# Hybrid decoder trunk on one core: the attention stage put in another order on TensorE, with its buffers moved to suit

## The chip, the cores and the metric

One core of one Trainium2 chip runs the whole program. The metric is the device time of one launch in microseconds (us), the median of three runs.

## The reference

Two pre-norm layers act on x of 256 tokens by 1024 channels, all in float32. In each layer, one projection of the normed x gives low-rank latents for multi-head latent attention (MLA: 8 heads, 96 wide queries and keys, 64 wide values), q, k and v of a dilated attention (3 groups of 8 heads, 64 wide), and two gates. Then

```python
merged = (jax.nn.sigmoid(g_mla) * (o_mla @ w_br_mla[i])
          + jax.nn.sigmoid(g_dil) * (o_dil @ w_br_dil[i]))
x = x + merged @ w_out[i]
```

Here o_mla is causal softmax attention, and o_dil is softmax attention over the three groups together with a distance bias. After it come a SwiGLU (layer 0) or the top 2 of 8 SwiGLU experts (layer 1), and a gated per-layer embedding. A last norm ends the program.

## The kernel before, in words

**Units.** All weights come from one stream in DRAM in the order in which they are used. SyncE loads slabs of 1 MB into six buffers (`raw`). A slab holds two units of 128 by 1024 numbers. ScalarE rounds each unit to fp32r (`hi`, L554), and VectorE writes what is left of it (`lo`, L925), each into a ring of four. A unit is then 12 TensorE matmuls of 512 columns (L1425 to L1427: high by high, high by low, low by high, for two blocks of 128 rows and both token tiles; with one token tile in the experts, six). ScalarE may round unit u only when TensorE has used unit u - 4 (`used`). Both engines take their work in program order, so a unit to be split can stand behind attention work, and the other way round.

**Attention stage of a layer** (the functions `attn` of each engine). The projections come first: latents, v (`U_V`), the MLA up-projections, then q and k of the dilated attention as six chunks of four units (`U_Q`, `U_K`). ScalarE copies each chunk to `chunk` (L661), TensorE transposes it in rounds (L1510), and VectorE copies the round to `qT` or `kT` (L1056). After all six chunks, 22 softmax batches follow: 6 of MLA (`NB_M`), 16 of the dilated attention. The latter come in pairs: token tile 0 with 128 keys per group, tile 1 with 256. For batch n:

- TensorE `scores(n)` (L1522, or nine matmuls of L1533 to L1535), in one of two score banks
- VectorE `prep(n)`: scale or bias, then the negated maximum `nmax` (L1082, L1086)
- ScalarE `exps(n)`: the exponentials and their sums (L672)
- TensorE `turn_probs(n)`: transposes of the probabilities (L1544)
- ScalarE `pt_evac(n)`: copies them to `pT` (L680, L682)
- TensorE `values(n)` (L1555, L1562)
- VectorE `normalise(n)` (L1099, L1100)

The loop on each engine runs a software pipeline: in step n TensorE does scores(n), then perhaps a gate unit, then turn_probs(n-1) and values(n-2). `exps(n)` waits for `oev` of n-2, that is for normalise(n-2), since the sums have two buffers. The 16 gate units (`U_G`) stand in the steps that the table `GATE_AT` names: four in MLA steps, then one in every second dilated step, the last ones behind. Four of them fill the two gate banks, and `gate_evac` on ScalarE (L696) must empty these before the next four. For the dilated scores q and k are split too, two heads' worth at a time (`round_pair`, L688 on ScalarE, `rest_pair` on VectorE; the table `SPLIT_AT`).

Then both outputs are transposed (L1591) and split (`omT`, `odT`), eight branch units multiply them (`U_BM`, `U_BD`), VectorE multiplies by the gates' sigmoids (L1135), GpSimd adds the two branches (L522), TensorE transposes `merged`, and the eight units of the output projection (`U_O`) follow.

**Memory.** Small tiles are laid one after the other; behind them lie regions (`qk_odd`, `Dr`, `Mr`, `Tr`) in which the stages' tiles overlay each other. In the program before, the regions start 64 bytes behind a multiple of 128.

## Time and profile before

| | us |
|---|---|
| three runs, median (lowest to highest) | 2065.55 (2065.05 to 2072.18) |
| the profiled execution | 2059.12 |
| its span | 2057.4 |
| PE busy | 1961.5 (95%) |
| DVE busy | 1497.9 (73%) |
| ACT busy | 1242.8 (60%) |
| POOL busy | 68.5 (3%) |
| chain that ended last, share of PE | 90% |
| TensorE's granted clock, mean | 0.959 of full speed |

PE is TensorE, DVE VectorE, ACT ScalarE, POOL GpSimd. The span goes from the first to the last instruction. Busy time is the time in which at least one instruction of the engine ran; matmuls overlap each other, so it is less than the sum of their durations. The clock is what the chip granted TensorE: 1.00 is 2.4 GHz, 0.50 is 1.2 GHz, and a value between them is a mean over both. The median of the runs is 6.4 us above the profiled execution.

### The profile page before, as it was taken

What the parts mean: (1) busy time and instruction counts of PE and PEld (TensorE: products, weight loads), DVE (VectorE), ACT (ScalarE), POOL (GpSimd) and SP (SyncE); (2) the same over time, 40 slices, a digit from 0 to 9 for tenths busy, and PEclk for the clock granted to TensorE, in tenths of its full rate; (3) what the DMA queues carried; (4) which work ended last, traced back from release to release, by engine and by line L of the source; (5) the groups of instructions that cost most, each with busy time, mean ns of one, the idle gap of its engine ahead of it and who ended that gap; (6) DMA issues with size and microseconds to landing.
All of it is one profiled execution on the core that took longest, in us unless ns stands there. A gap on an engine that the chain in (4) does not pass through costs nothing.

```text
span 2057.4 us, 27403 instructions
## 1 busy us (share of the span) xinstructions
PE 1961.5 (95%) x9278; PEld 1633.5 (79%) x9278; DVE 1497.9 (73%) x1685; ACT 1242.8 (60%) x1543; POOL 68.5 (3%) x127
## 2 busy tenths in 40 slices
PE   6998999999999999999899999999999999999996
PEld 5887877788887887877688888888888888888875
DVE  4456447556666455545698999989999898998985
ACT  4545354444445544443577777777777777777764
POOL 2200001000001100001000000000000000000000
PEclk8999899999999997799799999999999999999998
DMA  6543114555554542124499998989989898998980
GB/s 252 192 183 110 54 62 169 194 183 183 184 183 167 213 160 75 42 81 141 185 359 349 352 369 329 367 338 353 371 324 366 339 355 342 352 368 340 351 324 31
DMA packets 70064, 498.61 MB, mean 242 GB/s; under 512 B 7872, under 2 KB 7872, under 8 KB 10096
## 3 DMA queue, kind: packets, MB, share of 16 engines
q1 hardware_dynamic: 68656, 493.39, 63.8%
q0 software_dynamic: 1344, 4.36, 0.7%
q8 instruction: 41, 0.67, 0.1%
q14 instruction: 23, 0.19, 0.0%
HBM read 496.67 MB, written 1.05 MB: 242 GB/s over the span
## 4 chain that ended last, share of the span: by engine, by line
PE 90%; DVE 3%; ACT 3%; issue 3%; DMA 1%; POOL 1%; ACTq 0%; DVEq 0%; SPq 0%; POOLq 0%
PE ps L1425 27%; PE ps L1427 26%; PE ps L1426 26%; PE ps L1562 2%; PE ps L1705 2%; PE ps L1544 1%; PE ps L1713 1%; DVE lo L925 1%; PE ps L1510 1%; ACT hi L554 1%; PE ps L1555 1%; PE ps L1533 0%; PE ps L1522 0%; ACT pT L682 0%; ACT pr L672 0%
## 5 line engine op out<-in xcount | busy, mean ns | idle before, releaser
L925 DVE TENSOR_TENSOR lo<-raw,hi 128x1024 fp32r<-128x1024 f32 (+1 forms) x936 | 1104.8, 1219 | 237.4 <-ACT hi L554 235.6
L554 ACT ACTIVATE hi<-raw 128x1024 fp32r<-128x1024 f32 (+1 forms) x936 | 969.1, 1053 | 395.3 <-PE ps L1427 381.6
L1425 PE MATMUL ps<-hi,hs_hi 128*128 128x512 f32 x896 | 360.6, 402 | 6.9 <-DVE lo L925 5.4
L1425 PE MATMUL ps<-hi,hT_hi 128*128 128x512 f32 (+1 forms) x832 | 344.2, 414 | 21.4 <-DVE lo L925 14.5
L1427 PE MATMUL ps<-hi,hs_lo 128*128 128x512 f32 x896 | 352.5, 393 | 0.0
L1426 PE MATMUL ps<-lo,hs_hi 128*128 128x512 f32 x896 | 349.9, 391 | 0.0
L1426 PE MATMUL ps<-lo,hT_hi 128*128 128x512 f32 (+1 forms) x832 | 335.9, 404 | 0.0
L1427 PE MATMUL ps<-hi,hT_lo 128*128 128x512 f32 (+1 forms) x832 | 335.3, 403 | 0.0
L1425 PEld LDWEIGHTS ps<-hi,hT_hi 128*128 128x128 f32 x832 | 166.8, 200 | 57.6 <-DVE lo L925 11.9
L1425 PEld LDWEIGHTS ps<-hi,hs_hi 128*128 128x128 f32 x896 | 169.1, 189 | 42.7 <-DVE lo L925 8.8
L1427 PEld LDWEIGHTS ps<-hi,hs_lo 128*128 128x128 f32 x896 | 168.9, 188 | 39.6
L1426 PEld LDWEIGHTS ps<-lo,hs_hi 128*128 128x128 f32 x896 | 169.1, 189 | 34.9
L1427 PEld LDWEIGHTS ps<-hi,hT_lo 128*128 128x128 f32 x832 | 166.7, 200 | 35.2
L1426 PEld LDWEIGHTS ps<-lo,hT_hi 128*128 128x128 f32 x832 | 167.2, 201 | 32.2
L1425 PE MATMUL ps<-hi,eaT_hi 128*128 128x512 f32 x448 | 177.8, 397 | 2.9 <-DVE eaT_lo L1383 2.9
L1427 PE MATMUL ps<-hi,eaT_lo 128*128 128x512 f32 x448 | 176.4, 394 | 0.0
L1426 PE MATMUL ps<-lo,eaT_hi 128*128 128x512 f32 x448 | 175.1, 391 | 0.0
L672 ACT ACTIVATE pr<-pr,nmax 128x384 f32<-128x384 f32 (+2 forms) x64 | 39.1, 612 | 130.2 <-DVE o_dil L1100 102.5
L1425 PEld LDWEIGHTS ps<-hi,eaT_hi 128*128 128x128 f32 x448 | 84.6, 189 | 20.2 <-DVE lo L925 3.1
L1427 PEld LDWEIGHTS ps<-hi,eaT_lo 128*128 128x128 f32 x448 | 84.6, 189 | 19.8
L1426 PEld LDWEIGHTS ps<-lo,eaT_hi 128*128 128x128 f32 x448 | 84.6, 189 | 18.6
L1099 DVE RECIPROCAL rsum<-sums 128x1 f32<-128x1 f32 (+2 forms) x44 | 7.2, 165 | 102.4 <-PE ps L1562 85.5
(270 smaller groups left out, 1866.4 us busy)
## 6 DMA issues: line engine op xcount, KB each, us to landing
raw<-in_stream SPq DMA_DIRECT2D x468, 1024.0 KB, 4.8
xs<-in_x SPq DMA_DIRECT2D x2, 512.0 KB, 7.0
gain<-in_ffn_norm POOLq DMA_DIRECT2D x2, 512.0 KB, 3.7
gain<-in_ple_norm POOLq DMA_DIRECT2D x2, 512.0 KB, 6.1
out_x<-hnat SPq DMA_DIRECT2D x4, 256.0 KB, 2.3
gain<-in_attn_norm SPq DMA_DIRECT2D x1, 512.0 KB, 5.2
pnat<-in_p POOLq DMA_DIRECT2D x2, 256.0 KB, 3.2
gain<-in_attn_norm POOLq DMA_DIRECT2D x1, 512.0 KB, 6.4
```

Source lines behind the costliest of these rows:

```text
L554: a.activation(dst, src, ACT.Copy).then_inc(hi_done, 1)
L672: ins = a.activation(v, v, ACT.Exp, bias=nmax[:, n % 2, h:h + 1], accum_out=sums[:, n % 2, h:h + 1])
L925: v.tensor_tensor(dst, src, h, ALU.subtract).then_inc(lo_done, 1)
L1425: pe.matmul(o, ah, wh[:, kk, :], start=(first and kk == 0), stop=False)
L1426: pe.matmul(o, ah, wl[:, kk, :], start=False, stop=False)
L1427: ins = pe.matmul(o, al, wh[:, kk, :], start=False, stop=(last and kk == nk - 1))
L1510: ins = pe.transpose(ps[0:m, 4 + 2 * (r % 2) + t, P * k:P * k + P], src[t][k], ident[:])
L1544: ins = pe.transpose(ps[:, 4 + k // 4, P * (k % 4):P * (k % 4) + P], pr[:, n % 2, P * k:P * k + P], ident[:])
L1555: ins = pe.matmul(ps[:, 6, 64 * h:64 * h + 64], pT[:, n % 2, (t + 1) * h + k, :], vm[:, k, h0 + h, :], start=(k == 0), stop=(k == t))
L1562: ins = pe.matmul(ps[:, 6, 0:64], pT[:, n % 2, (t + 1) * m + k, :], vd[:, k, hd:hd + 64], start=(m == 0 and k == 0), stop=(m == DG - 1 and ...
L1705: ins = pe.matmul(ps[:, banks[k // 4], P * (k % 4):P * (k % 4) + P], src[:, t, P * k:P * k + P], sel[:, t, :], start=(t == 0), stop=(t == ...
L1713: ins = pe.transpose(ps[:, 6, P * k:P * k + P], e_act[:, P * k:P * k + P], ident[:])
```

## The change

The same matmuls, transposes and copies are done, in another order and with other banks and buffers.

1. The six MLA batches move up between the units of the three `U_K` chunks: two units, then one batch's scores, transposes and values.
2. Each step of the dilated loop has one unit (`fill_unit`, table `FILL_AT`): the gate units 3 to 15, and then the first three MLA branch units. Gate units 0 to 2 stand ahead of the loop. The one step without a unit (`OM_AT`) transposes o_mla.
3. The sums have four buffers, so exps(n) waits for normalise(n-4). The two gate banks, the score banks and the branch banks are others.
4. `o_dil` is transposed in two halves, the branch units start singly, and VectorE, not GpSimd, adds the branches (`merge`). The output units start when half of `merged` has been split.
5. Every region begins at a multiple of 128 bytes, so the tiles in them lie 64 bytes further on.

Tables and memory:

```diff
-EV_OPS = [2] * 7 + [4, 4] + [2] * 9
-GATE_BANKS = (3, 7)
-BRANCH_BANKS = ((2, 6), (0, 1))
-EV_ACT = [sum(EV_OPS[:n + 1]) for n in range(18)]
+EV_OPS = [2] * 7 + [4, 4] + [2] * 10
+GATE_BANKS = (2, 3)
+BRANCH_BANKS = ((2, 3), (0, 1), (6, 7), (2, 3))
+EV_ACT = [sum(EV_OPS[:n + 1]) for n in range(19)]
...
-GATE_AT = {n + 2: n for n in range(4)}
-GATE_AT.update({NB_M + 2 + 2 * k: 4 + k for k in range(8)})
-GATE_AT[NB + 1] = 12
-
-SPLIT_AT = {2: 1, NB_M + 4: 2, NB_M + 8: 3}
+FILL_AT = {n: n - 3 for n in range(NB_M, NB_M + 13)}
+FILL_AT.update({NB_M + 14 + k: 16 + k for k in range(3)})
+OM_AT = NB_M + 13
+
+SPLIT_AT = {NB_M + 1: 1, NB_M + 4: 2, NB_M + 8: 3}
...
         def region(n):
+            top[0] = (top[0] + 127) // 128 * 128
             r = top[0]
...
-        sums = sb("sums", [P, 2, 4])
-        rsum = sb("rsum", [P, 2, 4])
+        sums = sb("sums", [P, 4, 4])
+        rsum = sb("rsum", [P, 4, 4])
...
-        omT_hi = at("omT_hi", [P, 4, S], F32R, Dr)
-        omT_lo = at("omT_lo", [P, 4, S], F32R, Dr + 4096)
+        omT_hi = at("omT_hi", [P, 4, 2, S], F32R, Dr)[:, :, 0, :]
+        omT_lo = at("omT_lo", [P, 4, 2, S], F32R, Dr + 12288)[:, :, 0, :]
         odT_hi = at("odT_hi", [P, 4, S], F32R, Dr + 8192)
-        odT_lo = at("odT_lo", [P, 4, S], F32R, Dr + 12288)
-        merged = at("merged", [P, T, D], F32, Dr + 16384)
+        odT_lo = at("odT_lo", [P, 4, S], F32R, Dr + 20480)
+        merged = at("merged", [P, T, D], F32, Dr + 24576)
```

GpSimd:

```diff
-                for c in range(2):
-                    for t in range(T):
-                        g.wait_ge(y.ev_vec, 4 + 2 * c + t + 1)
-                        m = merged[:, t, CH * c:CH * c + CH]
-                        g.tensor_tensor(m, m, gates[:, 1, t, CH * c:CH * c + CH], ALU.add).then_inc(y.madd, 1)
                 g.wait_ge(y.madd, 4)
-                g.wait_ge(y.ev_vec, 8)
```

ScalarE (the loops in full, of the helpers the lines that the steps name):

```diff
                 def exps(n):
                     a.wait_ge(y.smax, n + 1)
-                    if n >= 2:
-                        a.wait_ge(y.oev, n - 1)
+                    if n >= 4:
+                        a.wait_ge(y.oev, n - 3)
                     nh, w = (MLA_BATCHES[n][2], 128 * (MLA_BATCHES[n][0] + 1)) if n < NB_M else (
                         1, 3 * 128 * (DIL_BATCHES[n - NB_M][0] + 1))
                     for h in range(nh):
                         v = pr[:, n % 2, h * w:h * w + w]
                         ins = a.activation(v, v, ACT.Exp, bias=nmax[:, n % 2, h:h + 1],
-                                           accum_out=sums[:, n % 2, h:h + 1])
+                                           accum_out=sums[:, n % 4, h:h + 1])
                     ins.then_inc(y.prob, 1)
...
                 def pt_evac(n):
                     a.wait_ge(y.ptr, n + 1)
+                    if n >= 2:
+                        a.wait_ge(y.pv, n - 1)
                     nb = 4 if n < NB_M else 3 * (DIL_BATCHES[n - NB_M][0] + 1)
+                    bank = 7 if n < NB_M else 4
...
                 def gate_evac(j, func, sig):
 
+                    done(b + U_G + 4 * j + 3)
...
-                for n in range(NB + 2):
+                for j in range(3):
+                    split_to(b + U_Q + 4 * j + 7, **kw)
+                    chunk_evac(j)
+                for j in range(3, 6):
+                    u, n = b + U_Q + 4 * j, 2 * (j - 3)
+                    split_to(u + 6, **kw)
+                    exps(n)
+                    if n:
+                        pt_evac(n - 1)
+                    split_to(u + 7, **kw)
+                    chunk_evac(j)
+                    split_to(u + 8, **kw)
+                    exps(n + 1)
+                    pt_evac(n)
+                split_to(b + U_G + 5, **kw)
+                pt_evac(5)
+                a.wait_ge(y.tevac, 10)
+                round_pair(0)
+                split_to(b + U_G + 7, **kw)
+
+                for n in range(NB_M, NB + 1):
+                    x = FILL_AT.get(n - 1, 0)
+                    if x % 4 == 3 and x < 16:
+                        gate_evac(x // 4, ACT.Copy, y.ev_act)
                     if n < NB:
                         exps(n)
-                    if 1 <= n <= NB:
-                        if n >= 3:
-                            a.wait_ge(y.pv, n - 2)
+                    if n > NB_M:
                         pt_evac(n - 1)
-                    j = 3 if n == NB_M else GATE_AT.get(n, 0)
-                    if j % 4 == 3 and n >= NB_M:
-                        done(b + U_G + j)
-                        gate_evac(j // 4, ACT.Copy, y.ev_act)
-                    if n in GATE_AT:
-                        split_to(b + U_G + GATE_AT[n] + 5, **kw)
+                    if n == OM_AT:
+                        a.wait_ge(y.otr, 1)
+                        a.activation(tok_blocks(omT_hi, 4), pair_blocks(2), ACT.Copy).then_inc(y.ohi, 1)
+                    if n in FILL_AT:
+                        split_to(b + U_G + FILL_AT[n] + 5, **kw)
                     if n in SPLIT_AT:
                         round_pair(SPLIT_AT[n])
...
+                for k in range(2):
+                    a.wait_ge(y.otr, k + 2)
+                    a.activation(od_half(odT_hi, k), od_blocks(k), ACT.Copy).then_inc(y.ohi, 1)
+                a.wait_ge(y.ev_act, EV_ACT[18])
+                for k in range(2):
+                    for t in range(T):
+                        a.activation(gates[:, k, t, :], gates[:, k, t, :], ACT.Sigmoid).then_inc(y.gsig, 1)
+                    split_to(b + U_BD + 4 + k, **kw)
```

VectorE, from the end of the stage:

```diff
+                def omT_rest():
+
+                    v.wait_ge(y.ohi, 1)
+                    v.tensor_tensor(tok_blocks(omT_lo, 4), pair_blocks(2), tok_blocks(omT_hi, 4),
+                                    ALU.subtract).then_inc(y.olo, 1)
...
+                def merge(c):
+
+                    for t in range(T):
+                        v.wait_ge(y.ev_vec, 4 + 2 * c + t + 1)
+                        m = merged[:, t, CH * c:CH * c + CH]
+                        v.tensor_tensor(m, m, gates[:, 1, t, CH * c:CH * c + CH], ALU.add).then_inc(y.madd, 1)
...
+                branch(0, 0)
+                split_to(b + U_BD + 4, dyn)
+                branch(1, 1)
+                split_to(b + U_BD + 5, dyn)
+                branch(2, 0)
+                merge(0)
+                split_to(b + U_BD + 6, dyn)
+                merged_rest(0)
+                split_to(b + U_BD + 7, dyn)
+                branch(3, 1)
+                merge(1)
+                split_to(b + U_BD + 8, dyn)
+                merged_rest(1)
 
                 split_to(b + U_O + 7, dyn)
```

TensorE:

```diff
+                def fill_unit(x):
+
+                    if x < 16:
+                        if x % 4 == 0 and x:
+                            evacuated(14 + x // 4)
+                        unit(b + U_G + x, dyn, hT_hi, hT_lo, (2, CH), 2 * (x % 4), GATE_BANKS, 0, x % 4 == 0, x % 4 == 3)
+                    else:
+                        k = x - 16
+                        unit(b + U_BM + k, dyn, omT_hi, omT_lo, (2, CH), 2 * (k % 2), BRANCH_BANKS[k // 2], 0, k % 2 == 0, k % 2 == 1)
+
...
+                for j in range(3, 6):
+                    evacuated((10, 12, 13)[j - 3])
+                    for h in range(4):
+                        unit(b + U_Q + 4 * j + h, dyn, hT_hi, hT_lo, (2, CH), 2 * h, (0, 1), 0, h == 0, h == 3)
+                        if h == 2:
+                            turn_round(j + 3, "qk", j - 1)
+                        if h % 2 == 1:
+                            n = 2 * (j - 3) + h // 2
+                            if n == 0:
+                                pe.wait_ge(y.tevac, 6)
+                                evacuated(11)
+                            scores(n)
+                            if n >= 1:
+                                turn_probs(n - 1)
+                            if n >= 2:
+                                values(n - 2)
+                pe.wait_ge(y.smax, NB_M)
+                fill_unit(0)
+                turn_probs(5)
+                values(4)
+                turn_round(9, "qk", 5)
+                fill_unit(1)
+                values(5)
+                fill_unit(2)
+
+                for n in range(NB_M, NB + 2):
                     if n < NB:
                         scores(n)
-                    if n in GATE_AT:
-                        gate_unit(GATE_AT[n])
-                    if 1 <= n <= NB:
+                    if n == OM_AT:
+                        evacuated(18)
+                        for t in range(T):
+                            for m in range(4):
+                                ins = pe.transpose(ps[:, 2 + t, P * m:P * m + P], o_mla[:, t, P * m:P * m + P], ident[:])
+                        ins.then_inc(y.otr, 1)
+                    if n in FILL_AT:
+                        x = FILL_AT[n]
+                        if x == 16:
+                            pe.wait_ge(y.olo, 1)
+                        if x == 18:
+                            pe.wait_ge(y.smax, NB)
+                        fill_unit(x)
+                    if NB_M < n <= NB:
                         turn_probs(n - 1)
-                    if n >= 2:
+                    if n >= NB_M + 2:
                         values(n - 2)
-                gate_unit(13)
-
+                    if n == NB:
+                        o_dil_turn(0)
                 pe.wait_ge(y.oev, NB)
-                pe.wait_ge(y.smax, NB)
-                for k, (src, b0) in enumerate(((o_mla, 4), (o_dil, 0))):
-                    for t in range(T):
-                        for m in range(4):
-                            ins = pe.transpose(ps[:, b0 + t, P * m:P * m + P], src[:, t, P * m:P * m + P], ident[:])
-                    ins.then_inc(y.otr, 1)
-                gate_unit(14)
-                gate_unit(15)
+                o_dil_turn(1)
+                fill_unit(19)
                 pe.wait_ge(y.olo, 2)
-                for k in range(4):
-                    if k >= 2:
-                        pe.wait_ge(y.ev_vec, 2 * (k - 1))
-                    lh, ll = ((omT_hi, omT_lo), (odT_hi, odT_lo))[k // 2]
-                    cols(b + U_BM + 2 * k, dyn, lh, ll, BRANCH_BANKS[k % 2], nku=2, units=2)
-
-                turn_tiles(merged, y.mtr, y.madd, 0)
+                unit(b + U_BD, dyn, odT_hi, odT_lo, (2, CH), 0, BRANCH_BANKS[2], 0, True, False)
+                pe.wait_ge(y.olo, 3)
+                unit(b + U_BD + 1, dyn, odT_hi, odT_lo, (2, CH), 2, BRANCH_BANKS[2], 0, False, True)
+                pe.wait_ge(y.ev_vec, 2)
+                unit(b + U_BD + 2, dyn, odT_hi, odT_lo, (2, CH), 0, BRANCH_BANKS[3], 0, True, False)
+                turn_tiles(merged, y.mtr, y.madd, 0, (0, 1))
+                unit(b + U_BD + 3, dyn, odT_hi, odT_lo, (2, CH), 2, BRANCH_BANKS[3], 0, False, True)
+
+                pe.wait_ge(y.ev_vec, 4)
+                pe.wait_ge(y.mlo, 2)
+                for h in range(4):
+                    if h == 1:
+                        turn_tiles(merged, y.mtr, y.madd, 0, (2, 3))
+                    if h == 2:
+                        pe.wait_ge(y.mlo, 4)
+                    unit(b + U_O + h, dyn, hT_hi, hT_lo, (2, CH), 2 * h, (0, 1), 0, h == 0, h == 3)
```

**The order, first place: TensorE in the dilated loop of layer 0, the end of the scores of a tile 1 batch.** Before, `pr` are probabilities, `vd` the values, `qk_hi` with `kT_lo` and `qT_lo` the split keys and queries:

```order
L1533 MATMUL ps<-qk_hi_105 128x256
L1534 MATMUL ps<-kT_lo,qk_hi_105 128x256
L1535 MATMUL ps<-qk_hi_105,qT_lo 128x256
L1544 MATMUL ps<-ident,pr 128x128 x3
L1562 MATMUL ps<-vd,pT 128x64 x6
L1533 MATMUL ps<-qk_hi_106 128x128
```

The scores are followed straight by the transposes of the batch before it. Now, at such a batch:

```order
L1612 MATMUL ps<-qk_hi_105 128x256
L1613 MATMUL ps<-kT_lo,qk_hi_105 128x256
L1614 MATMUL ps<-qk_hi_105,qT_lo 128x256
L1508 MATMUL ps<-hi,hT_hi 128x512
L1509 MATMUL ps<-lo,hT_hi 128x512
L1510 MATMUL ps<-hi,hT_lo 128x512
```

A unit (`hi`, `lo`, the activations `hT`) has come between the scores and the transposes.

**Second place: ScalarE in the dilated loop, around the second evacuation of the gate banks.** Before (`gates<-ps,rx` is the evacuation; here it is the first, the others stand likewise behind `pT`):

```order
L672 ACTIVATE pr,sums<-pr,nmax 128x384
L682 ACTIVATE pT<-ps 128x512
L696 ACTIVATE gates<-ps,rx 128x512 x2
L672 ACTIVATE pr,sums<-pr,nmax 128x768
L682 ACTIVATE pT<-ps 128x384
```

Now, the second evacuation:

```order
L683 ACTIVATE pr,sums<-pr,nmax 128x384
L694 ACTIVATE pT<-ps 128x256
L696 ACTIVATE pT<-ps 128x512
L564 ACTIVATE hi<-raw 128x1024
L702 ACTIVATE qk_hi_105<-qT 128x768
L702 ACTIVATE qk_hi_105<-kT 128x768
L708 ACTIVATE gates<-ps,rx 128x512 x2
L683 ACTIVATE pr,sums<-pr,nmax 128x768
```

The evacuation now stands behind a unit's split and both copies of `round_pair`; so does the third one.

**Third place: TensorE at `OM_AT`.** Now (the rows of before had nothing like it inside the loop):

```order
L1614 MATMUL ps<-qk_hi_106,qT_lo 128x256
L1706 MATMUL ps<-ident,o_mla 128x128 x8
L1624 MATMUL ps<-ident,pr 128x128 x3
L1642 MATMUL ps<-vd,pT 128x64 x6
L1612 MATMUL ps<-qk_hi_106 128x128
```

The transposes of o_mla have come into the loop, in a step without a unit.

## Rows read from the trace of the kernel before

**Rows 1.** Stretches: us, busy us of each engine (instructions), clock, DMA share, GB/s

```profile
165.00:345.00 180.00, 164.01 (x883) 140.39 (x882) 101.29 (x179) 86.70 (x158) 6.79 (x5) 0.91 0.25 90
...
770.00:950.00 180.00, 165.74 (x832) 142.01 (x831) 94.85 (x171) 81.00 (x150) 8.29 (x7) 0.83 0.24 83
1015.00:2030.00 1015.00, 1000.81 (x4601) 823.21 (x4599) 922.73 (x905) 767.06 (x829) 2.19 (x2) 0.99 0.90 342
```

**Rows 2.** Timeline of PE: start, us, what; layer 0's stage begins and ends, then layer 1's

```profile
168.65 1.04 PE L1510 MATMUL ps<-ident,chunk 128*128 128x128 f32 x8
...
326.05 1.04 PE L1445 MATMUL ps<-ident,merged 128*128 128x128 f32 x8
...
771.73 1.03 PE L1510 MATMUL ps<-ident,chunk 128*128 128x128 f32 x8
...
939.31 1.04 PE L1445 MATMUL ps<-ident,merged 128*128 128x128 f32 x8
```

**Rows 3.** Waits of PE, layer 0: waited for, us in total, times, longest

```profile
PE ps L1544 <- ACT pr L672: 2.5, 1, 2.5
...
PE ps L1544 <- ACT pT L682: 7.3, 8, 1.2
...
PE ps L1445 <- POOL merged L522: 1.8, 2, 1.3
PE ps L1425 <- ACT gates L696: 1.6, 1, 1.6
```

**Rows 4.** Timeline of PE in a pair of dilated batches, from turn to turn

```profile
233.58 0.82 PE L1544 MATMUL ps<-ident,pr 128*128 128x128 f32 x6
234.24 0.78 PE L1562 MATMUL ps<-vd,pT 128*128 128x64 f32 x6
234.94 0.38 PE L1533 MATMUL ps<-qk_hi 64*128 64x256 f32 x1
...
237.18 0.52 PE L1544 MATMUL ps<-ident,pr 128*128 128x128 f32 x3 [0.89 <-ACT pT L682]
237.53 1.45 PE L1562 MATMUL ps<-vd,pT 128*128 128x64 f32 x12
238.91 0.32 PE L1533 MATMUL ps<-qk_hi 64*128 64x128 f32 x1
...
242.92 0.82 PE L1544 MATMUL ps<-ident,pr 128*128 128x128 f32 x6
```

**Rows 5.** Stretches of layer 0 around a fall of the clock, and in the MLA batches

```profile
212.50:216.00 3.50, 2.60 (x23) 2.36 (x22) 2.34 (x6) 2.12 (x5) 0.00 (x0) 1.00 0.02 5
216.00:219.50 3.50, 3.50 (x13) 2.90 (x13) 2.36 (x6) 1.40 (x3) 0.00 (x0) 0.56 0.00 0
...
180.00:197.00 17.00, 17.00 (x100) 14.81 (x98) 10.85 (x18) 10.00 (x21) 0.00 (x0) 1.00 0.23 66
```

**Rows 6.** Timeline of ACT at the last pair of layer 0

```profile
288.06 0.59 ACT L682 ACTIVATE pT<-ps 128x512 f32<-128x512 f32 x1
288.53 1.27 ACT L696 ACTIVATE gates<-ps,rx 128x512 f32<-128x512 f32 x2
289.67 1.07 ACT L554 ACTIVATE hi<-raw 128x1024 fp32r<-128x1024 f32 x1
...
298.07 1.01 ACT L718 ACTIVATE omT_hi<-ps 128x1024 fp32r<-128x1024 f32 x1
```

**Rows 7.** Groups: busy us, mean ns | idle before; the split of q, and of units

```profile
L925 DVE TENSOR_TENSOR lo<-raw,hi 128x1024 fp32r<-128x1024 f32 x924 | 1095.2, 1224 | 221.2 <-ACT hi L554 219.5
...
L688 ACT ACTIVATE qk_hi<-qT 128x768 fp32r<-128x768 f32 x8 | 6.7, 842 | 5.0 <-DVE kT L1056 5.0
```

**Rows 8.** Durations (min/median/max ns) of weight loads, from a region and from outside one

```profile
L1425 PEld LDWEIGHTS ps<-hi,hs_hi x896: 186/188/330, 996.7 to 1990.4; 128*128 128x128 f32 x180
...
L1425 PEld LDWEIGHTS ps<-hi,hT_hi x83: 187/188/190, 100.2 to 164.3; 128*128 128x128 f32 x83
```

203 lines of the change are left out of this document (112 added, 91 removed).

## The prediction

> **What bounds the kernel now.** Three views were read in this order: the page, the stretches, and PE's waits and timeline. PE is busy in nearly all of the span and holds 90% of the chain that ended last, so the time goes where PE idles or runs at the lower clock. The stretches show where that is [rows 1]. The experts (1015 to 2030 us) run at clock 0.99 with PE busy 1000.8 of 1015 us: nothing to win, and the diff leaves their order alone. The two attention stages are different. Layer 0's stretch of 180 us has PE idle for 180.0 - 164.0 = 16.0 us at clock 0.91, layer 1's for 180.0 - 165.7 = 14.3 us at 0.83.
>
> *What the clock costs.* A mean of 0.91 over 180 us is 180 x 0.09 = 16.2 us of full clock lost, 0.83 is 30.6. Not all of it is time, since PE also waits. The layers give the price, for they issue the same work: from the last chunk's transposes to those of `merged`, layer 0 takes 326.05 - 168.65 = 157.4 us, layer 1 939.31 - 771.73 = 167.6 [rows 2]. Layer 1 is 10.2 us longer with 1.7 us less idle time, so 14.4 us of lost clock cost about 11.9 us, or 0.83 us each. Both layers lose 46.8, worth **39 us**.
>
> *When it falls.* In the dilated batches a pair needs 242.92 - 233.58 = 9.34 us at full clock, and holds one unit (the 3 us between the last scores and the next turn); for the other 6.4 us PE has only transposes, values, narrow scores and a 0.9 us wait [rows 4]. At 212.5 to 216.0 PE was busy 2.60 of 3.50 us without a unit, and the next 3.5 us ran at 0.56, nearly all at the 1.2 GHz level [rows 5]. The MLA batches, each with a unit and no wait, kept PE busy for all of 180 to 197 at clock 1.00 [rows 5]. So what lowers the clock is a long stretch without a unit, above all with a wait in it. One fall is 3.5 us x 0.44 = 1.5 us of clock lost, or 1.3 us of time; 46.8 / 1.5 makes some 31 such falls in both layers, about 1.9 per dilated pair: many follow each other without a break.
>
> **The change, part by part.** PE's own work is the same number of matmuls and transposes, so at full clock its sum doesn't change.
>
> *MLA between the K units, and a unit in each dilated step.* The waits listed in [rows 3] go: 2.5 us for the first probabilities (the last four K units now run there), and 7.3 us for `pT` in the dilated steps (a unit of some 2.8 us follows each scores; ACT has that long to finish). The 1.6 us for the gate banks is the subject of the next point. The largest stretch without a unit shrinks from 6.4 us to 0.65 + 0.70 + 1.1 = 2.5 us (the turn, the values, the scores before the next unit) or 0.35 + 1.4 + 1.1 = 2.9 us [rows 4], built like the MLA batches that kept the clock.
>
> *Where the new order waits.* Gate unit 4 starts a new bank, as do 8 and 12, and now the very next step has to do it. Let T be the end of the fourth unit of a bank. PE is ready again at T + 2.45. ScalarE must end `pT` (T + 1.6: in [rows 6] it ends 0.29 + 0.59 us behind the six transposes, here at T + 0.65), split a unit (1.0, the step from row to row), for units 8 and 12 also copy `round_pair` twice (0.84 each [rows 7], 1.6 overlapped), and empty two banks (1.2 [rows 6]). That is T + 5.4, a wait of **3.0 us** at units 8 and 12. Without `round_pair` it is 1.4 at the o_mla transposes, which wait for the fourth evacuation. Unit 4 has neither turn nor values ahead of it (ready at T + 1.05, banks empty at T + 2.6): 1.6. The row of before for such a wait is 1.6 us [rows 3], for a bank evacuated without `round_pair`.
>
> *The o_mla turn.* Branch unit 0 needs omT split. ScalarE gets to it behind the gates (T + 3.8), exps (1.0) and `pT` (0.5), with waits for VectorE's prep; the copy takes 1.0 [rows 6] and the rest 1.2, as a unit's [rows 7]: about T + 9. PE's turns, values and scores end at T + 7.5: wait 1.5, and more than 9 us pass without a unit.
>
> *At the joints.* Gate unit 0 uses the last MLA scores' banks and waits for prep(5), which stands behind the split of the last K unit: 1.0 + 1.2 + 1.4 against 2.2 us of PE work, 1.5. The prior row nearest to it is the 2.5 us [rows 3]; the ends are 0 and 2.5. The last normalise before the second half of the o_dil turn: 0.7. Merging: PE waited 1.8 us for GpSimd [rows 3]; VectorE needs about 0.7 for a piece of 512 columns (estimated from 1.22 us for 1024 [rows 7]), but the first piece of `merged` is turned between the last two branch units, when only one unit covers sigmoid, branch and merge: 1.5 in total. Small ones in the K chunks: 0.7.
>
> Per layer this sums to 1.6 + 3.0 + 3.0 + 1.4 + 1.5 + 1.5 + 0.7 + 1.5 + 0.7 = 14.9 us. Both layers: 29.8, against 16.0 + 14.3 = 30.3 now. **Waits: no gain, -0.5 us.** They move from eight small places to five larger ones.
>
> *The clock.* Falls are to be expected where a wait lies in a stretch without a unit: around unit 4, at 8 and 12 (2.45 + 3.0 = 5.5 us, like the 6.4 of now), at o_mla (9 us, two or more), at unit 0 and at the o_dil turn. I take 1 + 1.5 + 1.5 + 2.5 + 0.5 + 0.5 = 7.5 per layer, 15 in both, at 1.3 us: 20. The bounds are 5 and the 31 of now. So the clock gives back 39 - 20 = **19 us**.
>
> A transpose may count less than a matmul here. All that the rows show is that stretches with transposes, values and scores, with a wait, go before a fall [rows 5]. The Trainium skill, page "TensorE: Matmul & The Clock Gate", section "Part 4: PE-mode transpose", says that transposes don't count as PE activity in the way matmuls do. By that rule the o_mla step, with eight transposes of its own, would fall once more per layer, and the sum would be about 3 us worse. No row separates the two.
>
> *What is hidden.* The branch sum on VectorE adds four pieces of 0.7 us per layer; VectorE is busy 101.3 of 180 us there [rows 1], and its place on the path is in the 1.5 above. With four sums buffers ScalarE no longer waits for normalise(n-2), a part of the 7.3 us. GpSimd's later DMAs start no later. The split of each unit stays three units ahead of PE, and SyncE's queue follows it in the same order. The regions move by 64 bytes: weight loads take 188 ns from `hs_hi`, in a region, and 188 from `hT_hi`, outside [rows 8], so I take 0. The bounds are from the 1 ns between their minima: 4599 loads in the experts' stretch [rows 1] x 1 ns, 4.6 us either way if all of it lay on the path; most of it overlaps matmuls.
>
> **Sum.** -0.5 - 19 = -19.5 us. The profiled execution goes from 2059.1 to 2039.6; it lies 6.4 us below the median, so the median goes from 2065.55 to **2046**.
>
> **The rivals.**
> *Full clock.* With a unit in each step the falls are only those at o_mla, 5 in all (6.5 us), and the new waits are a third shorter (-10): 2065.6 - 0.5 - 32.5 - 10 = 2023, from 2015 to 2033. For it: the MLA batches kept 1.00 [rows 5]. Against it: they had no waits. 0.23.
> *The clock stays as it is.* A fall needs little: the 212.5 to 216.0 stretch was busy at 74% [rows 5]. If the 3 us waits, the turn and the 2.5 to 2.9 us stretches still bring some 31 falls, the result is 2065, from 2058 to 2071. 0.18.
> *Slower: ScalarE becomes the bound of each step.* It now has a unit's split in every step, and exps(n+1) stands ahead of `pT`(n). If each of the 22 batches per layer made PE wait 1.2 us (the longest wait for `pT` now is 1.2 [rows 3]), that is 44 x 1.2 = 53 us against the 30 removed, with the clock as it is: 2088. It decides from 0.9 us per batch. Against it: a step is 5.5 us on PE and 1.0 + 1.0 + 0.9 us on ScalarE. 0.07.
> *The change doesn't do what it says*: the units come later than the table of steps has them, since each waits for its split, and the stretch comes out as now: 2065. Against it: the split stays three units ahead. 0.03.
>
> **How the numbers follow.** My forecast has the remaining 0.49, with a range of its own from 2034 to 2056: the falls between 8 and 24 (9 and 12 us either side), the waits ± 3. No change within 0.5% (10.3 us, about what a measurement of this kernel can tell) is 2055.2 to 2075.9. Faster: 0.47 of the forecast's 0.49, all 0.23 of full clock, 0.02 of an unchanged clock, 0.72. Same: 0.02 + 0.16 + 0.03, 0.21. Slower: 0.07. The range reaches from 2022, which leaves out 0.09 below, to 2065, which leaves out 0.07 of slower and some of the unchanged clock.
>
> **What would show it.** In the profile after: the clock of both attention stretches at 0.94 or more; no wait of `L1544` for `pT` in the dilated steps, with PE's pair at 11.3 us for two units; the waits for `gates` at about 3 us, twice per layer, and 1.5 us twice; one wait for omT_lo. The experts' stretch should still last 1015 us, with the same clock. It is wrong if the clock in the dilated steps stays near 0.8, if waits for gates are under 1 us or over 4, or if the experts' stretch changes by over 3 us.

## The result and the profile after

The changed kernel takes **2017.8 us** (median of 4 runs, 2013.9 to 2018.3), the kernel before 2065.3 beside it (2064.4 to 2072.2). The ratio is 0.9756, with a 95% interval from 0.9735 to 0.9776. The forecast was 2046 with a range from 2022 to 2065. The sign is right, but the gain of 47.5 us is 2.4 times the 19.5 of the forecast, and the time lies below the range.

The head of the page of the changed kernel:

```profile
span 2016.6 us, 27409 instructions
## 1 busy us (share of the span) xinstructions
PE 1926.6 (96%) x9278; PEld 1608.9 (80%) x9278; DVE 1495.2 (74%) x1695; ACT 1245.2 (62%) x1547; POOL 56.4 (3%) x119
```

To see where the 40.8 us of the span came from, both programs are cut at the same landmarks on PE: each attention stage from the last transposes of `knat` to the transposes of `hnat` behind it, and the experts. The stretches of the kernel before, then of the changed one (columns as in [rows 1]):

```profile
133.20:346.40 213.20, 197.16 (x1040) 168.12 (x1041) 119.66 (x194) 100.14 (x173) 6.79 (x5) 0.93 0.28 101
736.30:961.30 225.00, 210.71 (x1041) 179.51 (x1042) 119.65 (x195) 99.26 (x172) 8.29 (x7) 0.86 0.27 95
1015.00:1985.00 970.00, 966.64 (x4459) 796.05 (x4457) 893.48 (x872) 745.50 (x799) 0.00 (x0) 1.00 0.92 353
```

```profile
133.40:336.10 202.70, 190.69 (x1040) 161.56 (x1041) 119.35 (x199) 101.07 (x175) 0.73 (x1) 0.96 0.30 106
722.70:926.60 203.90, 191.90 (x1040) 162.53 (x1041) 118.73 (x200) 100.11 (x174) 2.26 (x3) 0.95 0.30 105
982.00:1944.00 962.00, 958.55 (x4458) 795.21 (x4457) 891.12 (x870) 745.82 (x799) 0.00 (x0) 1.00 0.92 355
```

The attention stages give 10.5 and 21.1 us, 31.6 of the 40.8. Their waits (length less PE's busy time) fall from 16.0 + 14.3 to 12.0 + 12.0 us, 6.3 less. The lost clock (length times what the clock of the row lacks to 1.00; two digits of clock make it uncertain by 1 us a row) falls from 14.9 + 31.5 = 46.4 to 8.1 + 10.2 = 18.3 us; the 25.3 us that the waits don't explain are its worth, 0.9 us for each us of it. The experts' stretch needs 8 us less for the same number of matmuls **at clock 1.00 in both**. The prediction had 0 there, with bounds of 4.6 us, and named a change of over 3 us as a sign that it is wrong. From the first to the last matmul on `hs_hi` it is 994.1 against 988.1 us, 6.1 less before rounding.

The waits of PE in layer 0's attention, after (waited for, us in total, times, longest); they answer to [rows 3]:

```profile
PE ps L1508 <- ACT gates L708: 6.4, 3, 2.7
PE ps L1508 <- DVE nmax L1103: 2.7, 1, 2.7
PE ps L1706 <- ACT gates L708: 1.2, 1, 1.2
PE ps L1508 <- DVE omT_lo L1141: 0.9, 1, 0.9
PE ps L1662 <- DVE o_dil L1127: 0.5, 1, 0.5
PE ps L1642 <- DVE o_dil L1127: 0.2, 1, 0.2
```

The 7.3 us for `pT`, the 2.5 for `pr` and the 1.8 for `merged` are gone; waits for `gates` and for the gate banks (`nmax`) take their place. The largest one, at gate unit 8, in ScalarE's timeline and in PE's:

```profile
223.15 0.38 ACT L694 ACTIVATE pT<-ps 128x256 f32<-128x256 f32 x1 [1.30 <-PE ps L1624]
223.43 0.59 ACT L696 ACTIVATE pT<-ps 128x512 f32<-128x512 f32 x1
223.90 1.06 ACT L564 ACTIVATE hi<-raw 128x1024 fp32r<-128x1024 f32 x1
224.85 0.84 ACT L702 ACTIVATE qk_hi<-qT 128x768 fp32r<-128x768 f32 x1
225.59 0.84 ACT L702 ACTIVATE qk_hi<-kT 128x768 fp32r<-128x768 f32 x1
226.32 1.26 ACT L708 ACTIVATE gates<-ps,rx 128x512 f32<-128x512 f32 x2
```

```profile
227.63 0.80 PE L1508 MATMUL ps<-hi,hT_hi 128*128 128x512 f32 x1 [2.65 <-ACT gates L708]
228.23 0.63 PE L1509 MATMUL ps<-lo,hT_hi 128*128 128x512 f32 x1
228.66 0.63 PE L1510 MATMUL ps<-hi,hT_lo 128*128 128x512 f32 x1
```

The two evacuations of the gate banks stand behind `pT`, a unit's split and the pair's rounding, as the prediction had it. The unit behind the wait runs at the 1.2 GHz level (clock 0.50 from 227.0 to 230.5): from its second matmul on they start 0.43 us apart and not 0.23.

### The profile page after: what moved, and what is told of

Its sections match the earlier page's. It is cut to its first block, busy times and chain, and to the rows that moved or that the text cites. A ratio compares the mean times of both kernels' runs of the same rounds, so it can differ in the third digit from the quotient of the medians.

```text
span 2016.6 us, 27409 instructions
## 1 busy us (share of the span) xinstructions
PE 1926.6 (96%) x9278; PEld 1608.9 (80%) x9278; DVE 1495.2 (74%) x1695; ACT 1245.2 (62%) x1547; POOL 56.4 (3%) x119
## 4 chain that ended last, share of the span: by engine, by line
PE 89%; DVE 4%; ACT 3%; issue 3%; DMA 1%; POOL 0%; ACTq 0%; DVEq 0%; SPq 0%; POOLq 0%
PE ps L1508 27%; PE ps L1510 26%; PE ps L1509 26%; PE ps L1842 2%; PE ps L1642 1%; PE ps L1850 1%; DVE lo L956 1%; PE ps L1624 1%; ACT hi L564 1%; PE ps L1588 1%; PE ps L1612 1%; PE ps L1528 0%; PE ps L1601 0%; PE ps L1635 0%; DMA raw<-in_stream 0%
## 5 line engine op out<-in xcount | busy, mean ns | idle before, releaser
L1508 PE MATMUL ps<-hi,hT_hi 128*128 128x512 f32 (+1 forms) x832 | 338.7, 407 | 36.7 <-DVE lo L956 14.5
L1510 PE MATMUL ps<-hi,hT_lo 128*128 128x512 f32 (+1 forms) x832 | 330.9, 398 | 0.0
L1509 PE MATMUL ps<-lo,hT_hi 128*128 128x512 f32 (+1 forms) x832 | 330.5, 397 | 0.0
```

What stands on the lines that cost most here:

```text
L1508: pe.matmul(o, ah, wh[:, kk, :], start=(first and kk == 0), stop=False)
L1509: pe.matmul(o, ah, wl[:, kk, :], start=False, stop=False)
L1510: ins = pe.matmul(o, al, wh[:, kk, :], start=False, stop=(last and kk == nk - 1))
```

## Experiments

Each time is the median, with its ratio to the kernel before in runs beside it; that kernel's median lay between 2064.3 and 2070.0 there.

### e1: the addresses alone

```diff
         krope = sb("krope", [P, T, ROPE])
+        top[0] += 64
         qk_odd = region(6144)
```

> The kernel before with one edit: 64 bytes are left free ahead of the regions, so that every region starts at a multiple of 128 bytes, as in the changed kernel; order, banks and buffers stay. Theory A (the start of the weights' tiles sets the interval of the matmuls): in the experts the interval of two matmuls falls from 0.229 to 0.227 us, the time is 5 to 10 us below the kernel before (ratio 0.995 to 0.9975), and 4502 matmuls of the experts take 968 us and not 976. Theory B (the prediction's own: the move is worth nothing, and the 6 us of the experts came from something else): 0 within 1.5 us, the interval stays at 0.229.

**2051.7 us**, ratio 0.9921 (0.9897 to 0.9944), some 16 us less by the ratio, more than the 5 to 10 expected. Its stretches, as cut above:

```profile
133.30:350.00 216.70, 201.35 (x1041) 172.23 (x1042) 119.95 (x194) 100.03 (x173) 6.77 (x5) 0.91 0.28 99
737.80:959.50 221.70, 206.42 (x1041) 176.10 (x1042) 119.47 (x195) 99.01 (x172) 8.27 (x7) 0.88 0.27 97
1015.00:1975.00 960.00, 956.56 (x4447) 793.41 (x4446) 889.75 (x869) 744.29 (x797) 0.00 (x0) 1.00 0.92 355
```

The attention stages are as before (438.4 against 438.2 us); the experts' matmuls start 0.227 us apart as in the changed kernel. From the first to the last matmul on `hs_hi` the experts take 985.6 us and not 994.1. Theory A holds in the experts, B falls. The profiled run lies 10.3 us below that of before; the rest of the 16 us by the medians is not located, and the kernel before alone ran from 2061.8 to 2074.7 beside it.

### e2 and e3: tiles of the changed kernel moved by 64 bytes, all regions or `hs` alone

```diff
# e2
         def region(n):
-            top[0] = (top[0] + 127) // 128 * 128
...
+        top[0] += 64
         qk_odd = region(6144)
# e3
-        hs_hi = at("hs_hi", [P, KD, P], F32R, Dr + 16384)
-        hs_lo = at("hs_lo", [P, KD, P], F32R, Dr + 20480)
+        hs_hi = at("hs_hi", [P, KD, P], F32R, Dr + 16384 + 64)
+        hs_lo = at("hs_lo", [P, KD, P], F32R, Dr + 20480 + 64)
```

(In e3 the tiles behind `hs_lo` move by 128 bytes. Both put `hs` 64 bytes above its place in the changed kernel; in the kernel before it lay 64 below that place. So neither is the address of before again.)

> The changed kernel with its regions put back to 64 past a multiple of 128 bytes; all else stays. Theory A: 5 to 10 us above the changed kernel (2023 to 2028), PE's busy time in the experts is back at 976 us. Theory B: 2017.8 within 1.5 us. A third reading (the move matters only where the clock is fallen) expects the same as B in the experts, which run at full clock, and a loss in the attention stages.

> The changed kernel in which only hs_hi and hs_lo, the weights of the experts' gate and up matmuls, start at 64 past a multiple of 128 bytes; everything else stays at multiples of 128. Theory A: the matmuls whose weights are hs_hi or hs_lo have intervals of 0.229 us, those with eaT_hi or eaT_lo stay at 0.227; about two thirds of the experts' loss comes back, 4 to 6 us above the changed kernel. Theory B: no matmul changes, 2017.8 within 1.5 us.

e2: **2040.8 us**, 0.9874 (0.9848 to 0.9899); e3: **2037.7 us**, 0.9857 (0.9827 to 0.9887). Both lose 20 to 23 us, more than e1 had won, and it lies in the experts: from the first to the last matmul on `hs_hi` they take 1009.4 and 1007.7 us, where the changed kernel takes 988.1. The matmuls start 0.2333 us apart, not 0.229: a slower third value. And in e3 the `eaT` matmuls slowed to 0.232 too, although `eaT` still lay at a multiple of 128 bytes. So "aligned to 128 or not" is not the rule, and theory A falls in that form.

### e10 to e12: which address counts

```diff
# e10, the lo tiles likewise, those between and behind by 512 or 1024 (e11: +320 for faT, +384 for hs, +704 for eaT)
+        faT_hi = at("faT_hi", [P, 4, S], F32R, Dr + 8192 + 384)
+        hs_hi = at("hs_hi", [P, KD, P], F32R, Dr + 16384 + 128)
+        eaT_hi = at("eaT_hi", [P, 4, P], F32R, Dr + 28672 + 512 + 256)
# e12: two 32-byte tiles, taken from behind, push hi, lo, xs and hT by 64; the regions stay
+        r2 = sb("r2", [P, T])
+        part = sb("part", [P, 2])
         hi = sb("hi", [P, RING, UNIT], F32R)
```

> The changed kernel with three families of weights' tiles started at other places within 512 bytes (the changed kernel has all of them at 128 past a multiple of 512): hs at 256, eaT at 384, faT at 0. Intervals of two matmuls seen so far, by the start of the weights' tile past a multiple of 512: 64 gives 0.229 us, 128 gives 0.227, 192 gives 0.233, 256 (eaT in e3) 0.232. Theory F (the start within 512 bytes decides, tile by tile): hs 0.232, faT and eaT values of their own between 0.227 and 0.234. Theory G (the start within 256 bytes decides): eaT 0.227, hs and faT 0.232. Theory B' (only whether all are aligned to 128): all 0.227.

> As e10 with hs at 0, eaT at 320 and faT at 448 past a multiple of 512 bytes. Theory F: values of their own. Theory G (256 bytes decide): hs 0.232, eaT 0.229 (as 64), faT 0.233 (as 192). Theory B': hs 0.227, eaT and faT slow.

> The changed kernel in which the tiles that the matmuls stream, hi and lo, and with them xs and hT, start 64 bytes later (at 192 past a multiple of 512), while the regions with hs, eaT, faT and odT stay at 128. Theory H (the weights' own start decides): matmuls with hs, eaT, faT stay at 0.227, those with hT go from 0.227 to 0.233. Theory I (the start of the weights relative to that of the streamed operand decides; before: -64 gives 0.229, 0 gives 0.227, +64 gives 0.233): hs, eaT and faT go to 0.229, hT stays at 0.227. Theory J (the streamed operand's own start decides as well): all slower.

One run each, **2038.9, 2034.0 and 2028.1 us**; the intervals matter here, not the times. In e12 the weights' tiles hs, eaT and faT were not moved, and their matmuls slowed to 0.229; those on `hT`, which moved with the streamed tiles, kept 0.2276. Ten matmuls in a row, the first and the last, from e12's timeline of PE, then from the changed kernel's (start, us):

```profile
1162.61 0.39 PE L1510 MATMUL ps<-hi,hs_lo 128*128 128x512 f32 x1
...
1164.67 0.39 PE L1510 MATMUL ps<-hi,hs_lo 128*128 128x512 f32 x1
```

```profile
1163.88 0.39 PE L1508 MATMUL ps<-hi,hs_hi 128*128 128x512 f32 x1
...
1165.92 0.39 PE L1508 MATMUL ps<-hi,hs_hi 128*128 128x512 f32 x1
```

Nine intervals take 2.06 us in the first and 2.04 in the second, a difference of little more than the rounding. The means over 90 to 2400 intervals tell them apart. By where the weights' tile starts less where `hi` starts, modulo 256 bytes (for rows of matmuls without a wait; in the single units of the dilated loop those on `hT` and `omT`, both at 0, average 0.229 to 0.230 in the changed kernel):

| start less that of `hi`, mod 256 | mean interval, us | seen in |
|---|---|---|
| 0 | 0.2265 to 0.2281 | after, e1, e9; hT in all, in the dense FFN; eaT in e10 (256 on) |
| 64 | 0.2327 to 0.2335 | e2, e4; hs in e3; faT in e11 |
| 128 | 0.2320 to 0.2328 | eaT in e3; hs and faT in e10; hs in e11 |
| 192 (that is -64) | 0.2289 to 0.2299 | before; e12; eaT in e11 |

Theory G had the modulus right: e10 and e11 gave all six of its values, and F and B' fall. Theory I had the reference right, the start of the weights relative to that of the streamed operand; the weights' own place (H) would have kept hs at 0.227 in e12 and slowed hT. The kernel before lay at 192, so it lost 0.002 us per matmul, and the change moved it to 0. The effect is not symmetric: weights that start 64 bytes lower than at 0 cost 6 to 8 us in the experts, 64 higher some 20.

### e4 and e9: the late norm factors alone, in the order of before

```diff
-        sums = sb("sums", [P, 2, 4])
-        rsum = sb("rsum", [P, 2, 4])
+        sums = sb("sums", [P, 4, 4])
+        rsum = sb("rsum", [P, 4, 4])
...
-                    if n >= 2:
-                        a.wait_ge(y.oev, n - 1)
+                    if n >= 4:
+                        a.wait_ge(y.oev, n - 3)
```

(and `n % 4` for `n % 2` where they are used; e4 keeps the regions 64 bytes behind a multiple of 128, e9 has them where the changed kernel has them.)

> The kernel before with four buffers for sums and rsum, so that the exponentials of a batch wait for the normalisation of the fourth batch back and not of the second; regions stay at 64 past a multiple of 128 bytes and the order stays. This is the late norm factors alone. Theory C (the falls of the clock belong to the steps without a unit of matmuls, whatever the waits are): waits shorter by at most 1 us a layer, the clock falls as often as before, 2063 to 2066. Theory D (the wait of PE for pr and pT, 0.9 us in each dilated step, is what lets the clock fall): these waits shrink, fewer falls, 2045 to 2058.

> The kernel before with four buffers for sums and rsum and the late wait, as in e4, but with its regions at the addresses of the changed kernel (multiples of 128 bytes). Order and banks stay those of the kernel before. In e4 the matmuls of the experts ran at intervals of 0.2333 us, in the changed kernel at 0.227: 1009 against 988 us. If address and late factors add up: e4's 2025.7 less about 21 to 24 us, 2002 to 2006, faster than the changed kernel (2017.8), so that the new order costs time once the late factors are there. If the order is worth what the diff suggests (gate units in every pair of steps, merging joined): 2018 or more.

e4: **2025.7 us**, 0.9798 (0.9769 to 0.9827), although its matmuls ran at the slow 0.2333. The larger `sums` and `rsum` push all that lies behind them by 64 bytes, from 192 to 0. To keep the regions 64 past a multiple of 128, e4 leaves another 64 bytes free, which puts the weights at 64. So in the changed kernel too it is the two larger buffers that move the tiles, and the new line in `region` moves nothing: e9 doesn't have that line, and its matmuls run at 0.227 to 0.228. e9: **1999.4 us**, 0.9674 (0.9650 to 0.9699). It is 2.6 us below the range in which the two effects add up. This small part of the change, in the old order, beats the whole change by 18 us. e9's attention stretches, the main part of its dilated loop in layer 0, and its waits there:

```profile
131.10:326.60 195.50, 187.33 (x1041) 160.43 (x1042) 118.78 (x194) 100.67 (x173) 6.77 (x5) 0.97 0.32 110
715.90:908.20 192.30, 184.13 (x1041) 158.19 (x1042) 118.23 (x195) 99.76 (x172) 8.27 (x7) 0.99 0.32 112
200.00:267.00 67.00, 65.13 (x442) 57.99 (x440) 42.64 (x105) 36.91 (x75) 0.00 (x0) 1.00 0.19 64
```

```profile
PE ps L1544 <- ACT pr L672: 2.5, 1, 2.5
PE ps L1445 <- POOL merged L522: 1.8, 2, 1.3
PE ps L1425 <- ACT gates L696: 1.6, 1, 1.6
PE ps L1522 <- DVE kT L1056: 1.3, 1, 1.3
PE ps L1510 <- ACT chunk L661: 0.6, 1, 0.6
PE ps L1544 <- ACT pT L682: 0.4, 1, 0.4
```

Against e1, which has the same addresses, the stages are 438.4 - 387.8 = 50.6 us shorter. The eight waits for `pT` [rows 3] have become one of 0.4; all waits fall by 30.6 - 16.3 = 14.3 us. The other 36.3 us are clock: lost were 19.5 + 26.6 = 46.1 us, now 5.9 + 1.9 = 7.8. The stretches without a unit are as long as in e1, less the wait, and from 200 to 267 us the clock stayed at 1.00 through all of them. Theory D holds, and by far more than it asked for; theory C, the steps without a unit whatever the waits, falls. The wait of 0.9 us for `pT` in each pair was what let the clock fall: 50.6 us went with 14.3 us of waits, over three times their length. Whether it is PE standing still that counts, or that the stretch between two units is 0.9 us longer, these runs don't separate.

The traces bear this out. The attention stages of the changed kernel hold seven falls, those of the kernel before and of e1 14 each, e9's four. Each begins during a wait of PE or at most about 3 us behind the end of one. Not every wait brings a fall: at gate unit 0 the change has the same 2.7 us in both layers, and only layer 1 falls there (773 us).

### e7: the late norm factors undone in the new order

```diff
-                    if n >= 4:
-                        a.wait_ge(y.oev, n - 3)
+                    if n >= 2:
+                        a.wait_ge(y.oev, n - 1)
```

> The changed kernel in which the exponentials again wait for the normalisation of the second batch back (the late norm factors undone in effect, buffers kept). If the late factors matter in the joined order: new waits of PE for pr of 0.3 to 0.9 us in the dilated steps, 4 to 20 us slower, 2022 to 2038, with more falls of the clock. If the unit of matmuls in each step covers the chain anyway: 2018 within 2 us.

**2039.0 us**, 0.9878 (0.9846 to 0.9910), 21 us slower than the changed kernel, just above the 2022 to 2038 expected. The waits for `pr` that were expected don't come; the delay comes out where PE waits anyway, for ScalarE's evacuations and for `omT_lo` (0.9 in the changed kernel):

```profile
PE ps L1508 <- ACT gates L708: 9.9, 3, 4.4
PE ps L1706 <- ACT gates L708: 2.9, 1, 2.9
PE ps L1508 <- DVE omT_lo L1141: 2.1, 1, 2.1
```

With e1, e9 and the changed kernel this makes a square, all four at the same addresses (us):

| | waits for normalise(n-2) | waits for normalise(n-4) |
|---|---|---|
| order of before | 2051.7 (e1) | 1999.4 (e9) |
| new order | 2039.0 (e7) | 2017.8 (the change) |

The runs of the four were not made side by side: beside e1 the kernel before had a median of 2070.0, beside e7 2064.3. By the ratios, the new order gains 0.9921 - 0.9878, 9 us, where the factors are early, with an uncertainty of about the same size, and **loses 17 us** where they are late (0.9756 - 0.9674, give or take some 7). The two attention stages together, from the traces, say the same: 438.4 us in e1, 430.3 in e7, 387.8 in e9, 406.6 in the change, so 8 gained and 19 lost.

### e5, e6, e8, e13: what the new order waits for

```diff
# e5: the pair's rounding one step later
-SPLIT_AT = {NB_M + 1: 1, NB_M + 4: 2, NB_M + 8: 3}
+SPLIT_AT = {NB_M + 1: 1, NB_M + 5: 2, NB_M + 9: 3}
# e6: the gate banks emptied right behind exps(n), ahead of pT and the split
-                    x = FILL_AT.get(n - 1, 0)
-                    if x % 4 == 3 and x < 16:
-                        gate_evac(x // 4, ACT.Copy, y.ev_act)
                     if n < NB:
                         exps(n)
+                    x = FILL_AT.get(n, 0)
+                    if x % 4 == 3 and x < 16:
+                        gate_evac(x // 4, ACT.Copy, y.ev_act)
# e8: e5 + e6, and on VectorE
-                    split_to(u + 8, dyn)
+                    if j < 5:
+                        split_to(u + 8, dyn)
                     prep(n + 1)
+                    if j == 5:
+                        split_to(u + 8, dyn)
# e13: e8, with the omT_hi copy ahead of exps(n) on ScalarE, and on VectorE
                         prep(n)
+                    if n == OM_AT:
+                        omT_rest()
                     if n >= NB_M + 2:
                         normalise(n - 2)
-                    if n == OM_AT:
-                        omT_rest()
```

> The changed kernel with the rounding of the next head pair one step later (steps 5 and 9 of the dilated part in place of 4 and 8). It no longer stands on ScalarE ahead of the evacuation of a gate chunk. Theory E (the 2.65 us waits of PE at gate units 8 and 12 are the evacuation queued behind the rounding, some 1.5 us each): these two waits fall to about 1.1 us, as at gate unit 4; 4 waits x 1.5 us in two layers, 6 us, and up to four falls of the clock (3.4 us at half clock, 1.7 to 3.4 us each) fewer: 2017.8 - 6 to - 14 = 2004 to 2012. Rival (the wait is set by VectorE's scores or by the exponentials): waits stay, 2017 to 2019. Rival, slower: the remainders of the pair on VectorE now come later and the scores of heads 4 and 6 wait for them, a new wait of 1 us or more at steps 8 and 12.

> The changed kernel with the evacuation of a gate chunk moved on ScalarE from the start of the next step to right behind the exponentials of its own step, where its unit has just ended. Theory E: the evacuation no longer waits for the rounding nor for the next scores: all three gate waits shrink, 1.12 + 2.65 + 2.65 us to at most 0.5 each, 2 x 5 = 10 us less, 2004 to 2010 with the falls saved. Rival: ScalarE now stands waiting for the end of the gate unit, the probabilities' evacuation comes later, and PE waits for pT instead, 0.5 to 1.5 us a gate chunk: 2014 to 2022.

> The changed kernel with both edits of the two runs before (rounding one step later, gate chunk evacuated early) and, on VectorE, prep of the last MLA batch ahead of the split of the last weight chunk. If the three remaining causes of PE's waits are right, the 12 us of waits a layer fall to about 5 and the clock falls only at the head of each attention stage: 1998 to 2008. If one wait only takes the place of another: within 4 us of the better of the two single edits.

> The kernel of e8 with one more move: omT_hi is written on ScalarE ahead of the exponentials and the probabilities' evacuation of its step, and omT_lo on VectorE ahead of the normalisation. In e8 PE waited 2.19 us for omT_lo in each layer, and 3.4 and 6.8 us at half clock follow this wait (266 to 273 and 840 to 850). If the wait is the queue ahead of omT_hi: it falls to about 1 us, 2.4 us in two layers, and the falls behind it go, 1.7 and 3.4 us more: 1984.8 - 2.4 - 5.1 = 1977, between 1975 and 1983. If the exponentials of the step are late now: a wait for pr of 0.7 us or more in their place, 1984 to 1987.

| | us | ratio to before | PE's waits, both attention stages | clock lost there |
|---|---|---|---|---|
| the change | 2017.8 | 0.9756 (0.9735 to 0.9776) | 24.0 | 18.3 |
| e5 | 2003.7 | 0.9702 (0.9669 to 0.9734) | 18.1 | 9.8 |
| e6 | 1994.7 | 0.9661 (0.9629 to 0.9693) | 11.6 | 9.7 |
| e8 | 1984.8 | 0.9614 (0.9582 to 0.9646) | 6.6 | 5.7 |
| e13 | **1979.0** | 0.9571 (0.9533 to 0.9609) | 2.3 | 0 |

e5 took 1.5 us off each of the waits at units 8 and 12, as theory E said, and came out at the edge of the 2004 to 2012 expected. e6 took away all waits for `gates` but 0.2 us and gave more than expected, in spite of one wait that grew; its list for layer 0:

```profile
PE ps L1508 <- DVE nmax L1103: 2.7, 1, 2.7
PE ps L1508 <- DVE omT_lo L1141: 2.2, 1, 2.2
PE ps L1662 <- DVE o_dil L1127: 0.5, 1, 0.5
PE ps L1508 <- ACT gates L708: 0.2, 1, 0.2
PE ps L1642 <- DVE o_dil L1127: 0.2, 1, 0.2
```

e8 is 13 us below the 1998 to 2008 expected: its reorder on VectorE brought the wait for `nmax` from 2.7 to 0.2 us, and 3.3 us of waits a layer are left where 5 were expected. Its last large wait was the 2.2 us for `omT_lo`, which e13 removed, in the middle of its range. e13's attention stretches are the shortest of all, at full clock and nearly without waits:

```profile
133.30:317.90 184.60, 183.45 (x1041) 156.50 (x1042) 119.31 (x199) 101.47 (x175) 0.73 (x1) 1.00 0.33 117
705.60:890.20 184.60, 183.45 (x1041) 156.46 (x1042) 118.61 (x200) 100.52 (x174) 2.25 (x3) 1.00 0.34 116
```

The four edits move no work between engines. They put ScalarE's and VectorE's work in the order in which PE asks for it. e13 beats the kernel before by 4.3% and the change by 39 us. With it the new order is worth its trouble: 20 us better than e9, whose order still has the waits for `pr`, `merged` and `kT`. What the same care would do for the old order was not tried.

## Why the prediction was wrong

No single term makes the miss of 28 us. Waits, clock, experts and baseline are off by some 6 to 7 us each, all the same way, and the rest by 3. Behind one of them, the clock, stands a step that was wrong in its mechanism.

- **The waits (-0.5 us)**: right in place, a little off in size. Units 8 and 12 waited 2.65 us each (3.0 forecast), unit 4 1.1 (1.6), the o_mla transposes 1.2 (1.4), o_dil 0.7 (0.7). Gate unit 0 was undersized (2.7 against 1.5, and outside its ends of 0 and 2.5), omT oversized (0.9, forecast 1.5), and the merging and the K chunks, together 2.2 by forecast, cost nothing. A layer has 12.0 us in place of 14.9, 5.8 us less in both.
- **The clock (-19 us)**: the size was near. 28.1 us of lost clock went; 46.8 less 15 x 1.5 made 24.3 in the forecast. The price was 0.9 us for one us lost and not 0.83, so it gave 25.3 us: 6.3 more than forecast. Most falls also lie where they were put: in layer 0 at gate unit 4 (clock 0.52 from 203.0 to 206.5) and at units 8 and 12 (0.50 to 0.55 from 227.0 to 234.0 and from 254.5 to 261.5). At o_mla, where 2.5 per layer were forecast, there is none, which other runs of the same order don't repeat (see the last point).
- **The cause of that gain** is the step that failed: "what lowers the clock is a long stretch without a unit, above all with a wait in it". The fall needed the wait. e9 keeps the stretches without a unit, drops only the waits for `pT` (7.1 us a layer), and runs at 0.97 and 0.99. The late factors stood under what is hidden, as "a part of the 7.3 us", and had no share in the clock term. Yet at equal addresses they alone shorten the attention stages by 51 us in the old order, the new order alone by 8, and both together by 32. That the size of the clock term came near is luck: the gain of the late factors was larger than the forecast's, and the queues of the new order took a part of it back.
- **The regions (0, bounds 4.6 either way)**: mis-sized. The bound came from durations of weight loads [rows 8], a median of 188 ns in every kernel here, whatever the interval. What changed is the distance from one matmul's start to the next, 0.229 to 0.227 us, and since PE is busy all the while, no wait shows it. Why the interval moves, no run shows. It was worth 6 us from the first to the last `hs_hi` matmul (994.1 against 988.1) in the change, 8.5 in e1.
- **The baseline**: the profiled run of before lay 6.4 us under its median, that of the changed kernel 0.5 over its own. Carrying over the 6.4 added 6.9 us to the error.
- Together: 5.8 + 6.3 + 6.1 (experts) + 3.1 (the rest of the span, above all between the stages, where the clock went from 0.99 to 1.00 and the matmuls on `faT` gave 0.7) = 21.3 us in the profiled runs, and 6.9 for the baseline: 28 between 2046 and 2018.
- **The rivals**: 2023, "full clock", came nearest in time, though not by its mechanism: it had falls at o_mla alone and waits a third shorter, and the measured stages stand at 0.96 and 0.95 with 12.0 us of waits each and no fall at o_mla. "Slower: ScalarE becomes the bound" has its truth in the gate waits, each a queue on ScalarE, at four places and not at each step.
- **The transposes**: by the rule of the Trainium skill weighed in the prediction ("TensorE: Matmul & The Clock Gate", section "Part 4: PE-mode transpose"), the o_mla step should have fallen once more. In the changed kernel it kept 1.00, with a wait of 1.2 us ahead of the eight transposes and one of 0.9 behind them; PE was busy 2.56 of the 3.50 us of the second row:

```profile
281.50:285.00 3.50, 3.11 (x27) 3.04 (x28) 1.81 (x5) 2.29 (x5) 0.00 (x0) 1.00 0.02 5
285.00:288.50 3.50, 2.56 (x15) 2.12 (x15) 3.12 (x7) 0.37 (x1) 0.00 (x0) 1.00 0.00 0
```

That does not speak against the rule, for the same step fell elsewhere. e2, e3, e5, e10, e11 and e12 pass it too, with the same 1.2 us ahead and 0.5 to 0.9 behind. Of the 14 passes, with the changed kernel's two, 7 hold a fall. e12, which only moves tiles by 64 bytes, has two in each layer; those of layer 0:

```profile
280.80:284.20 3.40, 3.17 (x16) 3.17 (x16) 1.32 (x3) 1.73 (x5) 0.00 (x0) 0.50 0.00 0
287.60:291.00 3.40, 3.40 (x10) 2.62 (x9) 1.53 (x5) 0.71 (x2) 0.00 (x0) 0.50 0.52 152
```

The first began in the wait, ahead of the first of the eight transposes (281.04 us), so they can't be its cause. The longer waits of e6, e7 and e8 (2.1 to 2.9 us) saw a fall in all 6 passes; e13 has the same transposes with no such wait, and no fall in its 2. So the waits matter at this step and the transposes alone brought no fall. What divides the 7 passes from the other 7 at equal waits stays open, and so does how much a transpose counts.

## What to carry to other kernels

Take the recurring small waits first: here a 0.9 us wait in every second step of a loop that uses PE thinly cost three times its length through the clock, and two more buffers for the sums removed it. Try each part of a joined change alone, since here the small part was worth more than the whole, and the large part needed its queues on ScalarE put in PE's order before it paid. Compare the starts of successive matmuls, not only durations and idle time, when tiles move in memory, and remember that a small buffer that grows moves every tile behind it.

## What the runs showed of the hardware

- The interval between streamed fp32r matmuls of 128x512 depends on where the weights' tile starts relative to the streamed one, modulo 256 bytes: 0.227 us at 0, 0.229 at 192, 0.232 at 128, 0.233 at 64. That is up to 2.8% of an interval from a 64-byte shift, at clock 1.00 and with no wait to be seen. The values at 64 and 128 come from three or four kernels each, two of which ran once. Why is not known. Distances that aren't multiples of 64 were not tried.
- The same sort of stage can lose its clock over waits of 0.9 us (e1: 0.91 and 0.88 over the stages), and keep it at 1.00 for 184.6 us with waits of 0.5 us at most (e13).
- In the attention stages of the 15 traces the clock fell 104 times in all, each time during a wait of PE of over 0.3 us or within about 3 us of the end of one.
- A wait of the same length at the same place brings a fall in one pass and none in another: at the o_mla step 7 of 14 passes fell with the same 1.2 us wait ahead.
